# Reordering the start of expert routing in a hybrid attention and PEER kernel: meta gates, two projections, first sorts

## The chip, the cores and the metric

The kernel runs on one core of one Trainium2 chip. The metric is the device time of one execution in microseconds. A profile of one execution goes with it. Engines are named as in the profile: PE (matrix multiplications), DVE (vector), ACT (activations), POOL (which here issues gathers by index and does small arithmetic) and SP (which issues plain DMAs).

## The reference

Two layers over 528 rows (16 meta rows ahead of 512 rows of x), 1024 columns. In each layer a mixer is added to the rows, and then a PEER feed-forward network. The first mixer has stick-breaking attention and a short convolution, the second a windowed mean. What the change touches is the PEER part of the first layer:

```
q = (hb @ w_query).reshape(t, 8, 2, 128)
s = einsum('thpc,phkc->thpk', q, keys)
sv, si = top_k(s, 16)
cand = sv[:, :, 0, :, None] + sv[:, :, 1, None, :]
top_s, top_pos = top_k(cand, 16)
idx, gate = expert numbers of top_pos, softmax(top_s)
act = gelu(einsum('tnd,td->tn', expert_u[idx], hb))
y = einsum('tn,tnd->td', gate * act, expert_v[idx])
```

Each of 528 tokens takes 8 heads times 16 experts, so 128 rows of u and 128 of v, in float32, from tables of 16384 experts in each layer.

## The kernel before, in words

**Tiles and gathers.** There is the meta tile of 16 tokens and four tiles of 128 tokens, in two layers; the meta rows are needed in the first layer only. u and v of an expert lie side by side in memory. One gather (L1736, `gather_pool`, POOL) fetches 128 rows of 8 KB, for a tile u and v of all 128 experts of one token, for the meta rows 8 experts of each of the 16 tokens. There are 16 gathers for the meta rows and 8 times 128 for the tiles, 1040 in all. A chunk is 16 of them (CHUNK, L30). They land in groups of cells, four early ones (`ring_early`) and two late ones (`ring_late`); a group holds 3 x 1024 columns and successive gathers share its middle, so gather n needs the dot of the last user of its group and the sum of the user before that (class Place, L86). While only four groups exist these are gathers n-4 and n-8. The late groups lie in memory that the mixer uses: they may be filled only behind `late_constants` (L599), which waits until all output projections of the mixer are done. It stands behind the 20th gather of tile 0 (EARLY_TILE_ROWS, L80).

**Dots, weights, sums.** For each gather DVE multiplies u with the normed token rows and adds along the row (L2027, `dots_vector`). Four gathers make a batch: gelu of their dots, times the gates, gives weights. For the first nine batches DVE does the arithmetic (L1947 to L1969), with one exponential on ACT (L1917); the weights of a batch come right behind the first dot of the next batch. ACT spreads a weight into columns (L1927, `columns_scalar`), and PE adds v times weight (L1822 for the meta rows, L1861 for tiles; `meta_sums_tensor`, `sums_tensor`).

**The order of the work.** Every engine has one program in order, written by hand; engines wait for each other by semaphores. Work of other kinds is hung into these loops as hooks: a pair (row, step) lets an engine do the step behind its own instruction for that row. Routing one tile takes four pieces of two heads: PE multiplies a query (L1361), ACT copies it (L1368), PE transposes it (L1374), ACT copies (L1379), PE multiplies with the keys (L1452), and DVE sorts in 13 stages (`topk_stages`, L1456 on), the longest being the one-hot comparison (L1534). `piece_indices` (L1567) then writes the expert numbers of the piece, `piece_exponentials` (ACT, L1578) and `piece_gates` (DVE, L1584) make its gates.

**The start, where the change lies.** PE ends the attention and projects the mixer's output in eight half tiles, `project_tensor` 2 to 5 ahead of the meta sums and 6 to 9 step by step as hooks of the meta sums and of tile 0 (`project_step`, L935). DVE adds products 2 and 3 to the rows of tile 0 (L953), ACT takes 4 to 9 (`take_projected`, L957). DVE sorts the meta rows; PE selects by a small multiplication the indices and later the gates of the meta rows into the layout of the gathers (`meta_select_tensor`, L1425); DVE copies them (`meta_indices_vector` L1431, `meta_gates_vector` L1435). The indices go into a corner of one PSUM bank (QUERY_BANK, which query 1 fills later), the gates into another corner of the same bank. Then tile 0 is normed (L1276 to L1298, result hb), transposed (L1354), copied (L1289) and its first two pieces are queried and scored (`first_query`). The first two sorts are hooks of DVE's meta rows and of tile 0, the third and fourth follow as hooks too (META_QUERIED, L2132).

The two programs' lines around the change, PE and DVE before the meta loop:

```
meta_select_tensor(pe, top_i, META_IDX, s_midx)
project_tensor(pe, 3)
project_tensor(pe, 4)
start_tensor(pe, 1, P, 0)
```

```
dots_vector(dve, None, 0, [(0, lambda: meta_gates_vector(dve))] + of_chunk(early, 0) + ...)
```

Of the kernel before, what the change touches and what calls it, by code (L numbers as in the profile page):

```python
# [14 lines left out]
P = 128  # L15
# [102 lines left out]
def program(nc, x, x_T, x_cat, meta_tokens, mixer_small, even_w_in, even_w_out, odd_norm_g, odd_pool_w, odd_pool_scale, ffn_norm_g, peer_w_query,  # L118
# [3 lines left out]
    with ctx:  # L122
# [1300 lines left out]
        META_IDX, META_GATE = QUERY_BANK[:, 0:TOPK], QUERY_BANK[:, TOPK:2 * TOPK]  # L1423
# [615 lines left out]
        def tile_of(slot, n=P):  # L2039
            return hres[0:n, bass.ds(slot, 1), :].rearrange("p a d -> p (a d)")  # L2040
# [92 lines left out]
        SECOND_SORT = 8  # L2133
# [51 lines left out]
        def _(act):  # L2185
# [12 lines left out]
            take_projected(act, 4)  # L2198
            first_query(1)
            take_projected(act, 5)  # L2200
# [24 lines left out]
            def iteration(j, start=()):  # L2225
# [4 lines left out]
            columns_scalar(act, None, 0, [(4, first_indices), (5, lambda: piece_exponentials(act, 0)),   # L2230
                                          (5, lambda: take_projected(act, 6)), (10, lambda: take_projected(act, 7)),
                                          (12, lambda: stage_gates(act, 1, 1))] +
# [3 lines left out]
                  (4, lambda: piece_exponentials(act, 1)), (22, lambda: norm_scalar(act, 2, P, tile_of(1))),  # L2236
# [14 lines left out]
        def _(dve):  # L2251
# [8 lines left out]
            dve.wait_ge(s_meta_rows, 1)  # L2260
            logits_vector(dve, 0, P, 2)
            dve.wait_ge(s_v_in, HEAD_PAIRS)
            meta_indices_vector(dve)
            gates_vector(dve, 0, P, 2)
# [8 lines left out]
            def iteration(j, layer, start=()):  # L2273
# [5 lines left out]
            early = ([(i // 2, first[i]) for i in range(TOPK_STAGES)] + [(7, lambda: piece_indices(dve, 0))] +  # L2279
# [3 lines left out]
            dots_vector(dve, None, 0, [(0, lambda: meta_gates_vector(dve))] + of_chunk(early, 0) + [(11, lambda: piece_gates(dve, 0))])  # L2283
            tile(0, [(at - CHUNK, f) for at, f in early if at >= CHUNK] +
                 [(9, lambda: piece_gates(dve, 1)), (28, lambda: norm_vector(dve, 2, P, tile_of(1), 0)),
# [13 lines left out]
        def _(pe):  # L2299
# [5 lines left out]
            meta_select_tensor(pe, top_i, META_IDX, s_midx)  # L2305
            project_tensor(pe, 3)
            project_tensor(pe, 4)
# [3 lines left out]
            def first_query(s):  # L2311
                query_tensor(pe, first_piece(1) + s, s, P, 0, KD, (LATE_BANK, QUERY_BANK)[s])
                if s == 0:
                    pe.wait_ge(s_gate, 1)
                    meta_select_tensor(pe, soft, META_GATE, s_gateT)
                queryT_tensor(pe, first_piece(1) + s, P)
                pe.wait_ge(s_read, first_piece(1) + s)
                scores_tensor(pe, first_piece(1) + s, s, P)
            first_query(0)
            pe.wait_ge(s_idx, 1)  # L2320
            pe.wait_ge(s_mgate, 1)
            first_query(1)
            project_tensor(pe, 5)
# [59 lines left out]
```

## Time and profile before

| | |
|---|---|
| median of 3 runs | 3003.5 us (3002.41 to 3005.78) |
| the profiled execution | 3006.1 us, of which the span shown is 3004.3 us |
| PE, DVE, POOL, ACT busy | 63%, 62%, 46%, 27% of the span |
| moved by DMA | 1140 MB, of which 1091 MB by the gathers |
| mean granted clock of PE | 0.775 of full speed |

The time of an execution is a little more than the span between its first and last instruction on the engines. The profile counts us from the start of the span. A share of busy time is a mean over stages of different kinds: a table by stretches, and timelines of single engines, tell where something waits. In a timeline the last bracket of a line is how long the engine sat idle ahead of it and who released it. Merged lines give the number of instructions (x). Numbers of the weight loads of PE (PEld) lie beside its multiplications.

### The profile page before, as it was taken

How to read it: one execution, taken by the hardware profiler on the slowest of the kernel's cores; microseconds unless marked ns; L12 is line 12 of the kernel's file. 1: busy time of each engine (PE TensorE's matmuls, PEld its weight loads, DVE VectorE, ACT ScalarE, POOL GpSimd, SP SyncE). 2: the span in 40 equal slices, each digit the busy share in tenths (PEclk: the TensorE clock that was granted, in tenths of full speed). 3: DMA queues.
4: the chain of work that ended last, by engine and by line, in shares of the span. 5: the costliest groups of instructions: out<-in, count | busy, mean ns of one | idle time of the engine just before them, and what ended most of it. 6: DMA issues, size and time to landing. Idle time of an engine off the chain costs nothing. (4 is left out here: it accounts for less than half of the span.)

```text
span 3004.3 us, 41799 instructions
## 1 busy us (share of the span) xinstructions
PE 1888.3 (63%) x13330; PEld 765.0 (25%) x13330; DVE 1858.6 (62%) x4622; ACT 810.2 (27%) x3258; POOL 1369.0 (46%) x2651
## 2 busy tenths in 40 slices
PE   9999866746664566455665566566655666444444
PEld 4774322212221222122222222222222222111111
DVE  2155667885776567565776567755776477644444
ACT  2033122223222222123222332232223322232223
POOL 0100235555555555345555554555555555545554
PEclk9999988877876687777786777777777777666665
DMA  5132689999999999999999999999999999999998
GB/s 193 62 133 112 219 344 418 420 420 421 417 410 421 419 419 420 416 403 421 420 419 414 414 421 419 417 407 421 420 419 405 421 420 416 420 421 420 421 419 336
DMA packets 165496, 1140.19 MB, mean 380 GB/s; under 512 B 18672, under 2 KB 19696, under 8 KB 29856
## 3 DMA queue, kind: packets, MB, share of 16 engines
q0 software_dynamic: 149760, 1090.59, 88.1%
q1 hardware_dynamic: 15520, 46.94, 4.1%
q8 instruction: 109, 1.79, 0.2%
q14 instruction: 107, 0.88, 0.1%
HBM read 1135.30 MB, written 2.10 MB: 379 GB/s over the span
## 5 line engine op out<-in xcount | busy, mean ns | idle before, releaser
L2027 DVE SCALAR_TENSOR_TENSOR ring_early<-ring_early,psum 128x1024 f32<-128x1024 f32 x704 | 857.9, 1219 | 611.8 <-DMA ring_early<-in_peer_uv,idx_u 299.2
L1861 PE MATMUL psum<-ring_early,w_col 128*32 128x256 f32 x5504 | 541.2, 499 | 717.0 <-ACT w_col L1927 636.1
L2027 DVE SCALAR_TENSOR_TENSOR ring_late<-ring_late,psum 128x1024 f32<-128x1024 f32 x336 | 409.4, 1218 | 304.9 <-DMA ring_late<-in_peer_uv,idx_u 157.3
L1736 POOL DMA_INDIRECT ring_early<-in_peer_vu,idx_u x352 | 343.9, 977 | 468.3 <-DVE ring_early L2027 150.0
L1736 POOL DMA_INDIRECT ring_early<-in_peer_uv,idx_u x352 | 344.1, 978 | 427.9 <-DVE ring_early L2027 155.4
L1861 PE MATMUL psum<-ring_late,w_col 128*32 128x256 f32 x2688 | 271.3, 499 | 365.0 <-ACT w_col L1927 329.6
L1861 PEld LDWEIGHTS psum<-ring_early,w_col 128*32 128x32 f32 x5504 | 191.4, 133 | 1104.1 <-issue 737.8
L1919 ACT ACTIVATE ge<-ga 128x4 f32<-128x4 f32 (+2 forms) x256 | 52.5, 205 | 1403.9 <-POOL ga L1985 1403.9
L1927 ACT ACTIVATE w_col<-block_fold,weight 128x32 f32<-128x32 f32 x1024 | 268.9, 313 | 421.3 <-POOL weight L2001 395.4
L1361 PE MATMUL psum<-wq,hbT 128*128 128x512 f32 x512 | 314.7, 704 | 1.2 <-ACT hbT L1289 1.2
L1736 POOL DMA_INDIRECT ring_late<-in_peer_vu,idx_u x168 | 160.3, 954 | 267.7 <-PE psum L1861 152.2
L1861 PEld LDWEIGHTS psum<-ring_late,w_col 128*32 128x32 f32 x2688 | 93.4, 133 | 551.9 <-issue 343.7
L1736 POOL DMA_INDIRECT ring_late<-in_peer_uv,idx_u x168 | 168.3, 1002 | 113.6 <-issue 73.8
L1334 PE MATMUL psum<-hb_b,ident 128*32 128x512 f32 x768 | 152.5, 931 | 0.0
L1334 PE MATMUL psum<-hb,ident 128*32 128x512 f32 x768 | 138.4, 853 | 0.0
L1361 PEld LDWEIGHTS psum<-wq,hbT 128*128 128x128 f32 x512 | 84.9, 205 | 121.0 <-issue 119.6
L1902 ACT COPY gate_u<-gateT 32x8 f32<-32x8 f32 x512 | 99.1, 194 | 11.7
L1890 ACT COPY idx_u<-idxT 32x8 uint32<-32x8 uint32 x512 | 99.1, 194 | 11.6
L1083 POOL COPY vs<-qkv 128x640 f32<-128x640 f32 x4 | 2.9, 730 | 216.5 <-PE psum L760 122.6
L1334 PE MATMUL psum<-hres,ident 128*32 128x512 f32 x512 | 93.2, 861 | 0.0
L890 PE MATMUL psum<-hT,w_ring 128*128 128x264 f32 x384 | 87.0, 388 | 1.7 <-ACT qkv L989 1.7
L890 PEld LDWEIGHTS psum<-hT,w_ring 128*128 128x128 f32 x384 | 72.5, 190 | 15.0 <-ACT qkv L989 2.0
(294 smaller groups left out, 2221.4 us busy)
## 6 DMA issues: line engine op xcount, KB each, us to landing
wq<-in_peer_w_query SPq DMA_DIRECT2D x16, 1024.0 KB, 17.8
w_ring<-in_even_w_in SPq DMA_DIRECT2D x5, 2048.0 KB, 8.0
ring_early<-in_peer_vu,idx_u POOLq DMA_INDIRECT x352
ring_early<-in_peer_uv,idx_u POOLq DMA_INDIRECT x352
w_ring<-in_even_w_out SPq DMA_DIRECT2D x1, 4096.0 KB, 13.0
ring_late<-in_peer_vu,idx_u POOLq DMA_INDIRECT x168
ring_late<-in_peer_uv,idx_u POOLq DMA_INDIRECT x168
hT<-in_x_T SPq DMA_DIRECT2D x4, 528.0 KB, 6.7
```

The source lines that it names most:

```text
L890: last = nc.tensor.matmul(psum[:, 4 + 2 * (i % 2) + half, 0:HALF], w, hT[:, k, HALF * half:HALF * half + HALF], start=(k == 0), stop=(k == ...
L1083: nc.gpsimd.tensor_copy(vs[pair % 2][:, :, :], qkv[:, :, 2, 2 * DH * pair:2 * DH * pair + 2 * DH]).then_inc(s_v_in, 1)
L1334: nc.tensor.matmul(rows_for((f + 1) % 2)[BLOCK * g:BLOCK * g + BLOCK, c], ident[:, BLOCK * b:BLOCK * b + BLOCK], hb_of(job)[:, c], start=T ...
L1361: ins = nc.tensor.matmul(dst[0:n, :], hbT[:, k, 0:n], wq[:, k, bass.ts(s, 512)], start=(k == 0), stop=(k == KD - 1))
L1736: nc.gpsimd.indirect_dma_start(pair_cells(at), None, uv_rows if at.side else vu_rows, bass.IndirectOffsetOnAxis(idx_u[par][:, i:i + 1], 0) ...
L1861: nc.tensor.matmul(block_part(b, n), w_col[:, i % W_SLOTS, :], v_cell(at)[:, part_cols(n)], start=False, stop=last, skip_group_check=True) ...
L1890: nc.scalar.copy(cell, entry).then_inc(s_idx_u, 1)
L1902: nc.scalar.copy(cell, entry).then_inc(s_gate_u, 1)
L1919: nc.scalar.activation(ge[:, 0:n], ga[:, 0:n], ACT.Exp, scale=-GELU_B).then_inc(s_gact, 1)
L1927: nc.scalar.activation(w_col[:, i % W_SLOTS, 0:base.shape[-1]], base[:, :], ACT.Copy, scale=weight[par][:, i:i + 1]).then_inc(s_wcol, 1)
L2027: nc.vector.scalar_tensor_tensor(out=cell, in0=cell, scalar=1.0, in1=rows, op0=ALU.mult, op1=ALU.mult, accum_out=dot[par][:, i:i + 1]).the ...
```

## The change

It does six things. The gates of the meta rows go into the corner of the bank LATE_BANK. PE selects them right behind the indices, ahead of project 3, instead of in query 0 of tile 0, and waits for their copy ahead of query 0 instead of ahead of query 1. DVE makes the meta gates ahead of the copy of the indices and copies them right behind it, ahead of its additions, instead of as a hook of meta row 0; a wait for the repeated meta rows is dropped ahead of the logits (it stands again ahead of the dots). Project 4, which stood ahead of the transposes of tile 0, goes behind query 1, ahead of project 5; on ACT the two takings go from among the queries into the hooks of meta rows 0 and 1. DVE's first sort begins at row 3 instead of 0, and the second at 11 instead of 8. The hooks that hang on these sorts (the indices of tile 0's first chunk on ACT, exponentials and gates of pieces 0 and 1, staging of the gates) go some rows later.

```diff
--- before.py
+++ after.py
@@ -1420,7 +1420,7 @@
             act.wait_ge(s_q_ps, 1)
             nc.scalar.copy(q_T[:, :, :], FB.rearrange("p (a n) -> p a n", a=LISTS)).then_inc(s_qT, 1)
 
-        META_IDX, META_GATE = QUERY_BANK[:, 0:TOPK], QUERY_BANK[:, TOPK:2 * TOPK]
+        META_IDX, META_GATE = QUERY_BANK[:, 0:TOPK], LATE_BANK[:, 0:TOPK]
 
         def meta_select_tensor(pe, table, dst, done):
 
@@ -2130,7 +2130,8 @@
                     (at + 30, lambda: norm_vector(dve, job, P, src, 1))]
 
         META_QUERIED = (13, 29)
-        SECOND_SORT = 8
+        FIRST_SORT = 3
+        SECOND_SORT = FIRST_SORT + 8
         FIRST_QUERIED = (36, 50, 64, 78)
         FIRST_START = 92
 
@@ -2195,9 +2196,7 @@
             norm_scalar(act, 1, P, tile_of(0))
             transposed_scalar(act, 1, P)
             first_query(0)
-            take_projected(act, 4)
             first_query(1)
-            take_projected(act, 5)
 
             def first_indices():
                 act.wait_ge(s_piece, 1)
@@ -2227,13 +2226,14 @@
 
             act.wait_ge(s_setup, SETUP_STEPS)
             early = routing_scalar(act, 1, META_QUERIED, 2)
-            columns_scalar(act, None, 0, [(4, first_indices), (5, lambda: piece_exponentials(act, 0)), 
+            columns_scalar(act, None, 0, [(0, lambda: take_projected(act, 4)), (1, lambda: take_projected(act, 5)),
+                                          (7, first_indices), (9, lambda: piece_exponentials(act, 0)),
                                           (5, lambda: take_projected(act, 6)), (10, lambda: take_projected(act, 7)),
-                                          (12, lambda: stage_gates(act, 1, 1))] +
+                                          (15, lambda: stage_gates(act, 1, 1))] +
                            of_chunk(early, 0))
             tile(0, [(at - CHUNK, f) for at, f in early if at >= CHUNK] +
                  [(4, lambda: take_projected(act, 8)), (14, lambda: take_projected(act, 9)),
-                  (4, lambda: piece_exponentials(act, 1)), (22, lambda: norm_scalar(act, 2, P, tile_of(1))),
+                  (8, lambda: piece_exponentials(act, 1)), (22, lambda: norm_scalar(act, 2, P, tile_of(1))),
                   (24, lambda: piece_exponentials(act, 2)), (28, lambda: transposed_scalar(act, 2, P)),
                   (30, lambda: pool_norm_scalar(act, 0, 3, META, META_ROWS)),
                   (40, lambda: piece_exponentials(act, 3))] +
@@ -2257,11 +2257,11 @@
 
             for stage in topk_stages(dve, 0, 0, P, meta=True):
                 stage()
-            dve.wait_ge(s_meta_rows, 1)
             logits_vector(dve, 0, P, 2)
+            gates_vector(dve, 0, P, 2)
             dve.wait_ge(s_v_in, HEAD_PAIRS)
             meta_indices_vector(dve)
-            gates_vector(dve, 0, P, 2)
+            meta_gates_vector(dve)
             add_projected(dve, 2)
             add_projected(dve, 3)
             norm_vector(dve, 1, P, tile_of(0), 0)
@@ -2276,13 +2276,13 @@
             dve.wait_ge(s_meta_rows, 1)
             first = topk_stages(dve, first_piece(1), 0, P)
             second = topk_stages(dve, first_piece(1) + 1, 1, P)
-            early = ([(i // 2, first[i]) for i in range(TOPK_STAGES)] + [(7, lambda: piece_indices(dve, 0))] +
+            early = ([(FIRST_SORT + i // 2, first[i]) for i in range(TOPK_STAGES)] + [(FIRST_SORT + 7, lambda: piece_indices(dve, 0))] +
                      [(SECOND_SORT + i, second[i]) for i in range(TOPK_STAGES)] +
                      [(SECOND_SORT + TOPK_STAGES, lambda: piece_indices(dve, 1))] +
                      routing_vector(dve, 1, META_QUERIED, 2, piece_indices))
-            dots_vector(dve, None, 0, [(0, lambda: meta_gates_vector(dve))] + of_chunk(early, 0) + [(11, lambda: piece_gates(dve, 0))])
+            dots_vector(dve, None, 0, of_chunk(early, 0) + [(15, lambda: piece_gates(dve, 0))])
             tile(0, [(at - CHUNK, f) for at, f in early if at >= CHUNK] +
-                 [(9, lambda: piece_gates(dve, 1)), (28, lambda: norm_vector(dve, 2, P, tile_of(1), 0)),
+                 [(13, lambda: piece_gates(dve, 1)), (28, lambda: norm_vector(dve, 2, P, tile_of(1), 0)),
                   (32, lambda: piece_gates(dve, 2)), (37, lambda: pool_norm_vector(dve, 0, META, META_ROWS)),
                   (47, lambda: piece_gates(dve, 3))] +
                  routing_vector(dve, 2, FIRST_QUERIED) + tables_hooks(dve, 2, 0, 107) +
@@ -2303,23 +2303,22 @@
             meta_rows_tensor(pe)
             pe.wait_ge(s_routed, 2)
             meta_select_tensor(pe, top_i, META_IDX, s_midx)
+            pe.wait_ge(s_gate, 1)
+            meta_select_tensor(pe, soft, META_GATE, s_gateT)
             project_tensor(pe, 3)
-            project_tensor(pe, 4)
             start_tensor(pe, 1, P, 0)
             pe.wait_ge(s_hbT, 4)
 
             def first_query(s):
                 query_tensor(pe, first_piece(1) + s, s, P, 0, KD, (LATE_BANK, QUERY_BANK)[s])
-                if s == 0:
-                    pe.wait_ge(s_gate, 1)
-                    meta_select_tensor(pe, soft, META_GATE, s_gateT)
                 queryT_tensor(pe, first_piece(1) + s, P)
                 pe.wait_ge(s_read, first_piece(1) + s)
                 scores_tensor(pe, first_piece(1) + s, s, P)
+            pe.wait_ge(s_mgate, 1)
             first_query(0)
             pe.wait_ge(s_idx, 1)
-            pe.wait_ge(s_mgate, 1)
             first_query(1)
+            project_tensor(pe, 4)
             project_tensor(pe, 5)
 
             def tile(j, hooks):
```

## Rows read from the trace of the kernel before

**Rows 1.** The page's slices of the span, DMA's share in tenths.
```profile
DMA  5132689999999999999999999999999999999998
```

**Rows 2.** Stretches: busy us (count) of PE, PEld, DVE, ACT, POOL; clock, DMA, GB/s.
```profile
287.00:290.40 3.40, 3.40 (x6) 1.38 (x5) 0.46 (x1) 0.00 (x0) 2.23 (x3) 0.51 0.26 55
372.86:374.60 1.74, 1.74 (x17) 0.42 (x16) 1.71 (x9) 0.00 (x0) 0.86 (x1) 1.00 0.97 344
396.30:399.60 3.30, 3.30 (x24) 0.99 (x17) 2.43 (x6) 0.99 (x5) 0.95 (x1) 0.50 0.79 320
422.00:429.00 7.00, 6.54 (x54) 2.01 (x52) 5.37 (x18) 1.01 (x3) 1.89 (x2) 1.00 0.16 32
500.00:2990.00 2490.00, 1444.56 (x11024) 534.31 (x11012) 1606.27 (x3893) 685.15 (x2939) 1279.60 (x2487) 0.74 1.01 417
```

**Rows 3.** Timeline of POOL, 287 to 427: start, us, instruction, idle before and releaser.
```profile
287.56 1.20 POOL L1736 DMA_INDIRECT ring_early<-in_peer_vu,idx_u  x1 [53.64 <-ACT idx_u L1887]
...
301.57 0.94 POOL L1736 DMA_INDIRECT ring_early<-in_peer_uv,idx_u  x1 [9.08 <-DVE ring_early L2027]
...
321.30 0.94 POOL L1736 DMA_INDIRECT ring_early<-in_peer_uv,idx_u  x1 [18.80 <-DVE ring_early L2027]
...
337.15 1.17 POOL L1736 DMA_INDIRECT ring_early<-in_peer_vu,idx_u  x1 [9.10 <-PE psum L1822]
...
348.58 0.94 POOL L1736 DMA_INDIRECT ring_early<-in_peer_uv,idx_u  x1 [2.71 <-DVE ring_early L2027]
...
361.79 0.94 POOL L1736 DMA_INDIRECT ring_early<-in_peer_vu,idx_u  x1 [3.99 <-DVE ring_early L2027]
...
426.96 0.95 POOL L603 MEMSET prev<- 128x1024 f32 x1 [8.73 <-PE psum L944]
```

**Rows 4.** Timeline of PE, 285 to 426: merged runs of instructions.
```profile
285.44 0.62 PE L1428 MATMUL psum<-top_i,sel 128*128 128x16 f32 x4
285.91 8.81 PE L930 MATMUL psum<-w_ring,catT 128*128 128x512 f32 x16
...
303.33 1.04 PE L1354 MATMUL psum<-ident,hb 128*128 128x128 f32 x8
...
325.95 1.02 PE L928 MATMUL psum<-hres,ident 128*128 128x512 f32 x2
...
333.77 0.62 PE L1830 MATMUL psum<-hres,ident 16*16 16x256 f32 x8
...
335.67 0.62 PE L1822 MATMUL psum<-ring_early,w_col 128*16 128x256 f32 x8 [1.28 <-ACT w_col L1927]
...
347.10 0.63 PE L1822 MATMUL psum<-ring_early,w_col 128*16 128x256 f32 x8 [1.48 <-ACT w_col L1927]
...
360.21 0.63 PE L1822 MATMUL psum<-ring_early,w_col 128*16 128x256 f32 x8 [1.45 <-ACT w_col L1927]
...
395.71 0.64 PE L1861 MATMUL psum<-ring_early,w_col 128*32 128x256 f32 x8 [4.27 <-ACT w_col L1927]
396.14 3.58 PE L1334 MATMUL psum<-hb,ident 128*32 128x512 f32 x16
...
422.63 1.92 PE L1334 MATMUL psum<-hb,ident 128*32 128x512 f32 x16
...
425.88 1.02 PE L944 MATMUL psum<-w_ring,catT 128*128 128x512 f32 x2
```

**Rows 5.** Timeline of DVE, 286 to 358.
```profile
286.67 0.19 DVE L1613 TENSOR_TENSOR soft<-soft,soft_r 128x32 f32<-128x32 f32 x1
...
298.25 1.28 DVE L1298 SCALAR_TENSOR_TENSOR hb<-hres,rstd,ffn_g 128x1024 f32<-128x1024 f32 x1
...
313.05 0.17 DVE L1437 COPY gateT<-psum 128x16 f32<-128x16 f32 x1 [12.26 <-PE psum L1428]
...
319.30 1.22 DVE L2027 SCALAR_TENSOR_TENSOR ring_early<-ring_early,psum 128x1024 f32<-128x1024 f32 x1
...
357.93 1.22 DVE L2027 SCALAR_TENSOR_TENSOR ring_early<-ring_early,psum 128x1024 f32<-128x1024 f32 x1 [1.78 <-DMA ring_early<-in_peer_uv,idx_u]
```

## The prediction

> **What bounds the kernel now.** I read the slices of the page first. DMA is busy at 9 tenths from slice 7 to the end and nothing else is, so the expert rows that are fetched set the time there [rows 1]. A table of busy time by stretch says the same: from 500 to 2990 us the DMA engines move 417 GB/s at a share of 1.01 [rows 2]. Each gather brings 128 rows of 8 KB, 1.049 MB, so one takes 1.049 / 417 = 2.51 us there, and whatever happens to DVE, PE or POOL in that stretch costs nothing as long as the queue stays full. A change before it can only move the moment from which the queue is full. That moment is visible: from 422 to 429 DMA works at a share of 0.16, and in the timeline of POOL the last thing before the full stretch is the MEMSET of L603 at 426.96, which waited 8.73 us for PE L944, the last output projection [rows 2, 3]. Behind it 1004 of the 1040 gathers follow at the DMA's own pace (36 are issued before it). So the question is one number: how much earlier or later does PE finish that last product (425.88 + 1.02 = 426.9 [rows 4])? A shift there goes 1:1 into the time.
>
> I number gathers, dots and sums 0 to 15 for the meta rows and 16 on for tile 0. Gather n needs dot n-4 and sum n-8 (four cell groups). In POOL's timeline gather 4 is issued at 301.57, gather 5 waits 18.80 us for dot 1, gather 8 waits 9.10 us for PE's sum 0, and from there the gathers keep going [rows 3]. Dot 1 is late because DVE, right after dot 0, sits 12.26 us for the meta gates of PE and then does two stages of the first sort, until 319.30 [rows 5].
>
> **The change, part by part.**
> *Meta gates earlier.* PE does the second selection right behind the first. It now waits for the gates: their last DVE operation ended at 286.67 + 0.19 = 286.86, with the index copy ahead of it, and without that copy some 0.3 us sooner (two DVE operations of this size, 0.19 each), so 286.5 to 286.6 [rows 5]. Queued behind that wait on PE is project 3, which began at 285.91 [rows 4]. Selecting four matmuls costs 0.62 [rows 4], so project 3 begins at about 287.15, **+1.24**. The index copy itself goes behind the gates, at most 0.7 later, and with it gathers 0 to 3; dot 0 comes at about 300.8, some 13 us behind the first issue, so this is covered. Were it not, it would cost those 0.7.
>
> *DVE's wait goes.* Meta gates are copied near 287.3, so the 12.26 us are gone, and with the first sort moved to row 3, dots 1 to 3 follow dot 0 at 1.22 each. Gathers 5 to 7 are issued before 308 instead of at 321.30 and after. What is late next: gather 8, for sum 0. So these 18.80 us are worth nothing by themselves; their gain is only what they save behind gather 8.
>
> *The projections.* Before, project 4 ran while DVE and ACT made the normed rows of tile 0 (hb, ready at 298.25 + 1.28 = 299.53), and PE came to the transposes at 303.33 [rows 4, 5]. Now PE comes to them when hb is ready: 299.53 + 1.24 + 0.1 = 300.85. From the transposes to the start of project 5 the rows have 325.95 - 303.33 = 22.62 us; the selection inside it lay beside ACT's copy and its removal gives nothing. So the two queries end at 323.47, and now *two* projections follow, each as long as project 5 was, 333.77 - 325.95 = 7.82. The meta sum is opened (0.62, its last 0.06 under the next) at 339.1 and **sum 0 comes at 339.7 instead of 335.67: +4.0** [rows 4]. ACT's weights column 0 is ready long before, since it no longer stands behind project 5.
>
> *What of it is made up.* Between sum 0 and sum 8 PE waited 1.48 us at 347.10 and 1.45 at 360.21 for weights that needed dots 8 and 12 [rows 4]. PE without these waits needs 24.54 - 2.93 = 21.6, so sum 8 comes no sooner than 361.3, **+1.1**: the lower end. Upper end, if the row that dot 12 needs lands as slowly as before: sum 4 at 339.7 + 11.43 - 1.48 = 349.65, gather 12 behind it by 1.48 at 351.13, landing 357.93 - 348.58 = 9.35, and from dot 12 to sum 8 2.28: 362.8, +2.55 [rows 3 to 5]. I take +1.1, because the gathers before it now come at PE's even pace, 9.95 / 4 = 2.49 us a row, close to the DMA's own 2.51. From sum 8 on PE runs without a wait over its products and fills to the end of the meta rows; the next batches hang on landings of rows that hang on these sums. I take their spacing as before, so the shift stays.
>
> *The sorts.* First sort: its stages run while PE projects, when DVE has nothing else before row 8 lands. Second sort, three rows later: three stages fall into rows 20 to 22, where no sort stood. The longest stage takes 1.74 us [rows 2]. I cost it at nothing: dots there wait for landings. If that cover is gone, 3 x 1.74 = 5.2 at most. The moved exponentials and staged gates of tile 0 wait for nothing later than their new rows, and the ACT work of 1.7 us now behind row 15 lies beside PE's sum 15.
>
> *TensorE's clock.* The change makes PE idle: project 3 ends near 296.0, hb comes at 300.85, 4.9 us. The rows show such a case: after an idle of 4.27 us before 395.71 the granted clock was 0.50 from 396.30 to 399.60, which is the 1.2 GHz level, and the fill took 3.58 us where the one at 422.63 took 1.92 [rows 2, 4]. That is **+1.66** on the path, since transposes and query 0 follow directly. The bounds are 0 and that. I take it, 4.9 being longer than 4.27. The same table has a second fall: 0.51 from 287.00 to 290.40, inside project 3 (8.81 us), though PE had begun it at 285.91 and was busy in all of that stretch [rows 2, 4]. I leave 8.81 as it stands.
> The Trainium skill, in "TensorE: Matmul & The Clock Gate", section "Part 1: The HAM clock gate", gives the slow level to an idle engine and the full one to a busy one, and says that the point of change varies from run to run. Where the engine falls behind an idle stretch the trace agrees (0.50 after 4.27 us); the fall at 287.00 behind issued work it does not explain. By the page alone project 3 would run at full clock, 7.1 instead of 8.81, and the sum would be 1.7 lower.
>
> **Sum:** +1.1 + 1.66 = +2.8 us. The profiled execution has a span of 3004.3 and a time of 3006.1, 2.6 above the median of 3003.5; the shift is put on the median: **3006.3**.
>
> **Rivals.**
> - *The clock does not cost it* (no fall in the gap, or full clock in project 3 because PE's pattern differs): 1.7 less, 3004.6. For it: the fall at 287.00 came without an idle stretch, so the place of falls is not fixed. The page's rule above would give this time through project 3.
> - *Hidden anyway:* later batches have slack of 3 us and the gate stays at 426.9. For it: PE waits 4.27 at 395.71. Against it: that wait is for a landing of a row issued behind these sums. 3003.5.
> - *Faster batches:* from gather 8 at 337.15 to the MEMSET at 426.96, 28 gathers take 89.8 us, 3.2 each against 2.51, so a batch of four at full DMA pace saves 2.8 [rows 3]. If the freed DVE lets two batches do so: 4.0 - 5.6 = -1.6, 3001.9. With four: -7.2, 2996.3. Against it: the waits there are round trips (9.35 for a landing), not DVE work.
> - *Slower, by the second sort on DVE in rows 20 to 22:* +2.8 + 5.2 = +8.0, 3011.5. It decides as soon as dots 21 to 23 start behind a stage and not behind DMA. Before, dots of this stretch came behind DMA.
>
> **How the numbers follow.** A measurement of this kernel can tell about 0.2%, 6.0 us, from no change; that is 2997.5 to 3009.5. Forecast 0.45, clock 0.20, hidden 0.16, faster batches 0.09 (a third of it past 0.2%), slower 0.10. Of the forecast's cases with the upper landing bound (3007.8) a little also passes 3009.5 by scatter of the runs (3002.41 to 3005.78). So faster 0.04, same 0.86, slower 0.10. The range holds forecast with both bounds, clock, hidden and the two-batch case with the scatter: 3000.5 to 3010.0.
>
> **What would show it.** Right: gathers 5 to 7 issued before 310; PE idle some 5 us before the transposes of tile 0, and a half clock behind it; project 4 and 5 back to back and sum 0 near 339.7 to 341.4; the MEMSET of L603 near 429.7; 417 GB/s behind it. Wrong: a MEMSET before 426 (batches faster), or past 432 with dots 21 to 23 released by DVE itself; or a DMA that is not full behind the MEMSET, since then the end does not follow that point at all.

## The result and the profile after

| | before | after |
|---|---|---|
| median of 20 runs each | 3003.9 us (3000.16 to 3006.35) | 3008.68 us (3006.80 to 3011.34) |
| ratio, 95% interval | | 1.0018 (1.0012 to 1.0024) |
| profiled execution, its span | 3006.1, 3004.3 | 3007.9, 3006.1 |

The change costs 4.8 us, 0.18%; the interval reaches from 3.6 to 7.2 us. That lies within the 0.2% that the prediction called no change, at its edge, and inside its range; by the interval it is a loss and not a gain.

The timeline of POOL in the changed kernel, which answers to [rows 3]:

```profile
303.46 0.94 POOL L1736 DMA_INDIRECT ring_early<-in_peer_uv,idx_u  x1 [9.96 <-DVE ring_early L2027]
304.70 0.94 POOL L1736 DMA_INDIRECT ring_early<-in_peer_uv,idx_u  x1 [0.30 <-issue]
...
307.18 0.94 POOL L1736 DMA_INDIRECT ring_early<-in_peer_uv,idx_u  x1 [0.30 <-issue]
344.48 0.93 POOL L1736 DMA_INDIRECT ring_early<-in_peer_vu,idx_u  x1 [36.36 <-PE psum L1822]
...
366.05 0.93 POOL L1736 DMA_INDIRECT ring_early<-in_peer_vu,idx_u  x1 [2.49 <-PE psum L1822]
...
429.07 0.95 POOL L603 MEMSET prev<- 128x1024 f32 x1 [9.14 <-PE psum L944]
```

Gathers 4 to 7 now follow each other at 1.24 us, with no wait for another engine; the 18.80 us are gone. In their place gather 8 waits 36.36 us for PE, and it is issued at 344.48 instead of 337.15. Gather 16 is late by 4.3, the MEMSET by 2.1. All times of this run lie some 0.7 later from the start: the repetition of the meta rows on PE (L1444), ahead of everything that was changed, begins at 284.17 here and at 283.49 before. Below, times of different runs are compared from that instruction. In the kernel before it stands here, with query 0 of tile 0:

```profile
283.49 1.98 PE L1444 MATMUL psum<-ring_early,spread 16*128 16x512 f32 x4
...
305.53 7.13 PE L1361 MATMUL psum<-wq,hbT 128*128 128x512 f32 x16 [1.16 <-ACT hbT L1289]
```

The timeline of PE in the changed kernel, against [rows 4]:

```profile
284.17 1.98 PE L1444 MATMUL psum<-ring_early,spread 16*128 16x512 f32 x4
...
287.33 0.62 PE L1428 MATMUL psum<-soft,sel 128*128 128x16 f32 x4 [0.58 <-DVE soft L1613]
287.80 8.81 PE L930 MATMUL psum<-w_ring,catT 128*128 128x512 f32 x16
301.48 1.67 PE L1354 MATMUL psum<-ident,hb 128*128 128x128 f32 x8 [4.87 <-DVE hb L1298]
304.31 9.28 PE L1361 MATMUL psum<-wq,hbT 128*128 128x512 f32 x16 [1.16 <-ACT hbT L1289]
...
334.61 1.02 PE L928 MATMUL psum<-hres,ident 128*128 128x512 f32 x2
...
342.43 0.62 PE L1830 MATMUL psum<-hres,ident 16*16 16x256 f32 x8
342.98 0.62 PE L1822 MATMUL psum<-ring_early,w_col 128*16 128x256 f32 x8
...
352.86 0.62 PE L1822 MATMUL psum<-ring_early,w_col 128*16 128x256 f32 x8
...
364.45 0.62 PE L1822 MATMUL psum<-ring_early,w_col 128*16 128x256 f32 x8
...
398.50 0.64 PE L1861 MATMUL psum<-ring_early,w_col 128*32 128x256 f32 x8 [2.17 <-ACT w_col L1927]
```

The second selection waits 0.58 and project 3 begins 3.63 us behind L1444 instead of 2.42. Then the idle stretch, 4.87 us ahead of the transposes, and behind it transposes of 1.67 us (1.04 before) and a query 0 of 9.28 (7.13). Two projections stand ahead of the meta sums. Sum 0 begins 58.81 us behind L1444 instead of 52.18, **6.6 later**. The waits ahead of sums 4 and 8 (1.48 and 1.45 before) are gone.

The timeline of DVE in the changed kernel, against [rows 5]:

```profile
287.99 0.17 DVE L1437 COPY gateT<-psum 128x16 f32<-128x16 f32 x1 [0.62 <-PE psum L1428]
...
302.60 1.22 DVE L2027 SCALAR_TENSOR_TENSOR ring_early<-ring_early,psum 128x1024 f32<-128x1024 f32 x1
...
316.99 0.89 DVE L1511 MAX8 sv<-psum 128x8 f32<-128x128 f32 x4 [10.12 <-PE psum L1452]
...
325.90 0.17 DVE L1963 TENSOR_SCALAR ge<-ge 128x4 f32<-128x4 f32 x1 [4.37 <-ACT ge L1917]
...
349.93 1.22 DVE L2027 SCALAR_TENSOR_TENSOR ring_early<-ring_early,psum 128x1024 f32<-128x1024 f32 x1 [10.81 <-DMA ring_early<-in_peer_vu,idx_u]
...
389.44 1.21 DVE L2027 SCALAR_TENSOR_TENSOR ring_early<-ring_early,psum 128x1024 f32<-128x1024 f32 x1
...
394.25 1.21 DVE L2027 SCALAR_TENSOR_TENSOR ring_early<-ring_early,psum 128x1024 f32<-128x1024 f32 x1
```

Meta gates are copied at 287.99 instead of 313.05, and dot 1 comes at 302.60 instead of 319.30. DVE then waits where it did not wait before: 10.12 us for the scores of the first piece, 4.37 for ACT's first exponential, and 10.81 for the row of gather 8, which hangs on PE. The time that the dots won is spent waiting. The two last lines are dots 21 and 23: DVE had no idle time ahead of them, nor ahead of dot 22 between them, for they start behind stages of the second sort. In the kernel before dot 21 waited for its row:

```profile
384.85 1.22 DVE L2027 SCALAR_TENSOR_TENSOR ring_early<-ring_early,psum 128x1024 f32<-128x1024 f32 x1 [1.84 <-DMA ring_early<-in_peer_uv,idx_u]
```

The busy time by stretch of the changed kernel, columns as in [rows 2]:

```profile
296.70:301.40 4.70, 0.00 (x0) 0.00 (x0) 2.59 (x7) 1.65 (x4) 0.00 (x0) 1.00 0.98 404
301.90:308.60 6.70, 5.54 (x12) 2.68 (x10) 4.87 (x11) 1.07 (x2) 3.74 (x4) 0.50 0.54 171
...
500.00:2990.00 2490.00, 1446.86 (x11025) 536.88 (x11020) 1606.10 (x3892) 685.37 (x2939) 1277.51 (x2487) 0.74 1.01 418
```

PE does nothing from 296.7 to 301.4, and its granted clock is 0.50 from 301.9 to 308.6, the 1.2 GHz level. From 500 us on DMA moves 418 GB/s at a share of 1.01, where it was 417 and 1.01 before.

### The profile page after: what moved, and what is told of

It is laid out like the page before. It is cut to its first block and busy times, and to the rows that moved or that the text cites. A ratio compares the mean times of both kernels' runs of the same rounds, so it can differ in the third digit from the quotient of the medians.

```text
span 3006.1 us, 41797 instructions
## 1 busy us (share of the span) xinstructions
PE 1892.0 (63%) x13330; PEld 768.6 (26%) x13330; DVE 1858.8 (62%) x4622; ACT 810.5 (27%) x3258; POOL 1366.2 (45%) x2651
## 5 line engine op out<-in xcount | busy, mean ns | idle before, releaser
L1736 POOL DMA_INDIRECT ring_early<-in_peer_vu,idx_u x352 | 342.3, 973 | 492.8 <-PE psum L1861 156.2
L890 PE MATMUL psum<-hT,w_ring 128*128 128x264 f32 x384 | 87.0, 388 | 1.7 <-ACT qkv L989 1.7
L890 PEld LDWEIGHTS psum<-hT,w_ring 128*128 128x128 f32 x384 | 72.5, 190 | 15.0 <-ACT qkv L989 2.0
## 6 DMA issues: line engine op xcount, KB each, us to landing
w_ring<-in_even_w_out SPq DMA_DIRECT2D x1, 4096.0 KB, 12.9
```

The costliest lines, as they stand in the source:

```text
L890: last = nc.tensor.matmul(psum[:, 4 + 2 * (i % 2) + half, 0:HALF], w, hT[:, k, HALF * half:HALF * half + HALF], start=(k == 0), stop=(k == ...
L1736: nc.gpsimd.indirect_dma_start(pair_cells(at), None, uv_rows if at.side else vu_rows, bass.IndirectOffsetOnAxis(idx_u[par][:, i:i + 1], 0) ...
```

## The experiments

The theory going in: only the moment at which PE ends the last projection counts; the change makes it later by moving project 4 behind the queries, through the longer way to sum 0 and through the slow clock behind the idle stretch. Rivals: the later sorts slow DVE's batches; PE's wait for the gates ahead of project 3 is the loss.

**Project 4 ahead of the transposes again.** The changed kernel, on PE:

```diff
             project_tensor(pe, 3)
+            project_tensor(pe, 4)
             start_tensor(pe, 1, P, 0)
...
             first_query(1)
-            project_tensor(pe, 4)
             project_tensor(pe, 5)
```

> The changed kernel with project 4 alone put back ahead of the transposes of tile 0; the early gates and the late sorts stay. Theory (PE's order): the 4.87 us of idle PE and the slow clock behind it are gone, sum 0 comes near 336 to 337 instead of 343, the dots no longer hold anything up, so the MEMSET of L603 comes at 424 to 427.5 and the time is 3000 to 3004, that is 4.5 to 8.5 us under the changed kernel. Rival 1 (the late second sort slows the batches on DVE): the time stays within 1.5 us of 3008.7. Rival 2 (PE's wait for the gates ahead of project 3, +1.2): it stays 1 to 2 above before, 3005 to 3006.

Measured: 3001.6 us, ratio to before 0.9996 (0.9987 to 1.0005), so 7.1 under the changed kernel's 3008.7. The timelines of PE and of POOL:

```profile
305.18 1.04 PE L1354 MATMUL psum<-ident,hb 128*128 128x128 f32 x8
307.38 7.13 PE L1361 MATMUL psum<-wq,hbT 128*128 128x512 f32 x16 [1.16 <-ACT hbT L1289]
...
336.18 0.63 PE L1822 MATMUL psum<-ring_early,w_col 128*16 128x256 f32 x8
```

```profile
422.49 0.95 POOL L603 MEMSET prev<- 128x1024 f32 x1 [8.17 <-PE psum L944]
```

Transposes and query have their old durations, sum 0 comes 52.06 us behind L1444, and the MEMSET comes at 422.49. Early gates and late sorts are in this kernel, and the takings on ACT; together they do not make it slower than before. So neither rival is the cause of the loss. What the gates cost by themselves, which the takings hide here, is told below.

**Only project 4 moved.** The kernel before with this (ACT's two takings go with it, since query 1 and project 4 would else wait for each other):

```diff
-            take_projected(act, 4)
...
-            take_projected(act, 5)
...
-            columns_scalar(act, None, 0, [(4, first_indices), (5, lambda: piece_exponentials(act, 0)), 
+            columns_scalar(act, None, 0, [(0, lambda: take_projected(act, 4)), (1, lambda: take_projected(act, 5)),
+                                          (4, first_indices), (5, lambda: piece_exponentials(act, 0)),
...
-            project_tensor(pe, 4)
             start_tensor(pe, 1, P, 0)
...
             first_query(1)
+            project_tensor(pe, 4)
             project_tensor(pe, 5)
```

> The kernel before with project 4 alone moved behind query 1 (and its taking and that of project 5 moved on ACT); gates and sorts as before. Theory (PE's order): PE idles near 4.9 us behind project 3, the clock falls behind it, sum 0 comes at 339 to 342 and the time is 3006 to 3009. Rival 1 (sorts) and rival 2 (gates): neither is in this kernel, so 3003 to 3004.5.

Measured: 3006.5 us, 1.0012 (1.0003 to 1.0021). On PE:

```profile
300.20 1.97 PE L1354 MATMUL psum<-ident,hb 128*128 128x128 f32 x8 [4.87 <-DVE hb L1298]
303.33 9.45 PE L1361 MATMUL psum<-wq,hbT 128*128 128x512 f32 x16 [1.16 <-ACT hbT L1289]
```

PE idles 4.87 us, transposes and query take 1.97 and 9.45, sum 0 comes 58.07 behind L1444. That is 3.3 above before in the same comparison, without early gates and late sorts; the share of ACT's takings in it is seen below.

**The idle stretch filled.** The changed kernel with multiplications whose result nobody reads:

```diff
             project_tensor(pe, 3)
+            for k in range(5):
+                nc.tensor.matmul(FA, catT[:, k, META:META + P], w_out_sb[:, k, 0:512], start=True, stop=True)
             start_tensor(pe, 1, P, 0)
```

> The changed kernel with five multiplications of 128x512, whose result nobody reads, put into PE's idle stretch ahead of the transposes (some 4.4 us of work in 4.9 of idle). Only the clock behind the gap can change. Theory: the clock stays full, transposes and query 0 take 1.04 and 7.1 us instead of 1.67 and 9.28, sum 0 comes 2 to 2.8 us sooner and the time is 3006 to 3007. Rival (the clock costs nothing on the path): 3008 to 3009.5, as the changed kernel.

Measured: 3006.5 us, 1.0013 (1.0004 to 1.0022), 2.2 under the changed kernel and 2.3 under the next version, which has the changed kernel's time and ran in the same comparison. The same stretches and the way to sum 0:

```profile
296.70:301.40 4.70, 4.18 (x10) 1.52 (x8) 2.59 (x7) 1.65 (x4) 0.00 (x0) 1.00 1.01 415
301.90:308.60 6.70, 5.54 (x18) 2.67 (x17) 4.84 (x11) 1.07 (x2) 3.75 (x4) 1.00 0.54 177
```

```profile
301.45 1.09 PE L1354 MATMUL psum<-ident,hb 128*128 128x128 f32 x8 [0.57 <-DVE hb L1298]
303.71 7.13 PE L1361 MATMUL psum<-wq,hbT 128*128 128x512 f32 x16 [1.16 <-ACT hbT L1289]
...
340.23 0.62 PE L1822 MATMUL psum<-ring_early,w_col 128*16 128x256 f32 x8
```

With 4.18 us of work in the gap the clock is 1.00 behind it, the transposes take 1.09 and the query 7.13, and sum 0 comes 56.09 us behind L1444 instead of 58.81: the slow clock is 2.7 of the 6.6. The intervals of the two ratios overlap, so the time alone would not show it; the trace does. The rest of the 6.6 is project 4's place.

**Sorts and their hooks back.** The changed kernel with `FIRST_SORT = 0`, and the hooks that hang on it at their rows of before (4, 5 and 12 of the meta rows and 4 of tile 0 on ACT, 11 and 9 on DVE).

```diff
-        FIRST_SORT = 3
+        FIRST_SORT = 0
```

> The changed kernel with the first sort back at row 0, the second at row 8 and their hooks back where they were; gates and projections as changed. Theory (PE's order): dots 1 to 3 wait for the scores again, some 18 us, gathers 5 to 7 come near 320 and later, but gather 8 still waits for sum 0 near 343: the time stays within 1.5 us of the changed kernel, 3007 to 3010. Rival 1 (the late second sort): 3 us or more sooner, 3003 to 3005.5.

Measured: 3008.8 us, 1.0020 (1.0011 to 1.0029): the changed kernel's time. The timeline of POOL:

```profile
304.40 0.94 POOL L1736 DMA_INDIRECT ring_early<-in_peer_uv,idx_u  x1 [9.96 <-DVE ring_early L2027]
323.47 0.94 POOL L1736 DMA_INDIRECT ring_early<-in_peer_uv,idx_u  x1 [18.14 <-DVE ring_early L2027]
...
345.70 0.94 POOL L1736 DMA_INDIRECT ring_early<-in_peer_vu,idx_u  x1 [15.48 <-PE psum L1822]
```

Gather 5 waits 18.14 us again, and it costs nothing, since gather 8 still waits 15.48 for PE. The 18.80 us that the change removed were worth nothing, as the prediction had it.

**Project 4 cut into steps.** The changed kernel, with project 4's nine steps in PE's idle places. By its edit this version, and the version with gates in the idle stretch, multiplies tile 0's columns and rows there in place of tile 1's, in the same shapes; so it does not compute the kernel's result, and its time is that of the order alone.

`fourth(n)` issues one of them: the identity on the rows for n = 0, then one of the eight products.

```diff
             project_tensor(pe, 3)
+            for n in range(4):
+                fourth(n)
             start_tensor(pe, 1, P, 0)
+            fourth(4)
             pe.wait_ge(s_hbT, 4)
...
                 query_tensor(pe, first_piece(1) + s, s, P, 0, KD, (LATE_BANK, QUERY_BANK)[s])
+                fourth(5 + 2 * s)
                 queryT_tensor(pe, first_piece(1) + s, P)
+                fourth(6 + 2 * s)
...
-            project_tensor(pe, 4)
             project_tensor(pe, 5)
```

> The changed kernel with project 4 cut into its nine steps and put into PE's idle places: four steps while tile 0 is normed, one while ACT copies the transposes, one in each of the four waits of the two queries. Theory (only the start of the meta sums, and with it the MEMSET, sets the time): PE idles nowhere over 1 us, the clock stays full, sum 0 comes near 332.5 to 333.5 where project 4 ahead of the transposes gave 336.2, and the time is 2997 to 2999.5, the lowest so far. Rival (from there on DVE's sorts or the landings limit the batches, so an earlier sum 0 is worth nothing): 3001 to 3002, as with project 4 ahead of the transposes.

Measured: 2998.5 us, 0.9987 (0.9978 to 0.9996), with sum 0 48.37 us behind L1444, 3.7 sooner than with project 4 ahead of the transposes. The median is 2.7 to 3.1 under the two versions with project 4 ahead (3001.2 further down, 3001.6): an earlier sum 0 is worth most of its time, and nothing on DVE or in the landings takes its place yet.

**Project 4 ahead, sorts back.** The first experiment and the fourth together, so that of the change the early gates and ACT's takings are left.

```diff
             project_tensor(pe, 3)
+            project_tensor(pe, 4)
             start_tensor(pe, 1, P, 0)
...
-        FIRST_SORT = 3
+        FIRST_SORT = 0
```

> The changed kernel with project 4 ahead of the transposes and both sorts back at rows 0 and 8, so that the gates' early selection is what is left of the change (and the takings on ACT). Theory: dots 1 to 3 wait for the scores again, gathers 5 to 7 come after 320, and with sum 0 near 336 DVE's sort stages and dots of rows 5 to 8 now stand behind the weights: gathers 9 to 12 come later than with late sorts, 3003 to 3005. Rival (the sorts' place is worth nothing, whatever sum 0 does): 3001 to 3002.5, as with project 4 ahead and late sorts.

Measured: 3001.2 us, 0.9996 (0.9987 to 1.0005). The theory missed and the rival held: with sum 0 at its old place too, the place of the sorts is worth nothing that can be told (0.4 us apart). Gathers 5 to 7 come at 322.94 to 328.76, and gather 8 still waits 7.76 us for PE.

**Gates in the idle stretch.** As the version in steps, with the second selection behind project 3 and DVE's copy of the gates behind its second addition.

```diff
-            pe.wait_ge(s_gate, 1)
-            meta_select_tensor(pe, soft, META_GATE, s_gateT)
             project_tensor(pe, 3)
+            pe.wait_ge(s_gate, 1)
+            meta_select_tensor(pe, soft, META_GATE, s_gateT)
...
-            meta_gates_vector(dve)
             add_projected(dve, 2)
             add_projected(dve, 3)
+            meta_gates_vector(dve)
```

> As the version with project 4 in steps, but PE selects the meta gates behind project 3, in the idle stretch, and DVE copies them behind its second addition. Theory: PE's wait for the gates no longer stands ahead of project 3, which begins 1.2 us sooner, and the rest follows: 1.0 to 1.5 us under the version with project 4 in steps, 2996 to 2998.5. Rival (the 1.2 us are given back to the DMA or to ACT's norm): no difference, within 0.5.

Measured: 2995.9 us, 0.9977 (0.9968 to 0.9986), 2.6 under the version in steps where 1.0 to 1.5 was expected. Sum 0 comes 2.9 us sooner (45.48 behind L1444). 1.2 of it is the wait; the other 1.7 is a project 3 of 7.11 us instead of 8.81, as in the next.

**The same with tile 1's columns.** The wait for the rows of x goes to tile 1's with them.

```diff
-                    nc.tensor.matmul(late_bank(4), ident[:, :], hres[:, 0, 0:512], start=True, stop=False)
+                    nc.tensor.matmul(late_bank(4), ident[:, :], hres[:, 1, 0:512], start=True, stop=False)
...
-                ins = nc.tensor.matmul(late_bank(4), catT[:, n - 1, cols_of(0)], ...
+                ins = nc.tensor.matmul(late_bank(4), catT[:, n - 1, cols_of(1)], ...
```

> The version with the meta gates selected behind project 3 and project 4 in steps, now with tile 1's columns in project 4's steps (the two versions in steps above multiplied tile 0's there, in the same shapes). Theory: as measured with tile 0's columns, 2994 to 2998, the fastest kernel here, since only the start of the meta sums counts. Rival (the values matter for the time, by other expert numbers fetched): 3 us or more away from 2995.9.

Measured: 2996.4 us, 0.9977 (0.9968 to 0.9986): faster than both kernels, 12.3 under the changed one. The columns make no difference that can be told (2995.9 with tile 0's). The version in steps was not run again with tile 1's. The timelines of PE and of POOL:

```profile
284.29 1.98 PE L1444 MATMUL psum<-ring_early,spread 16*128 16x512 f32 x4
...
286.74 7.11 PE L930 MATMUL psum<-w_ring,catT 128*128 128x512 f32 x16
...
298.71 1.09 PE L1354 MATMUL psum<-ident,hb 128*128 128x128 f32 x8 [0.38 <-DVE hb L1298]
```

```profile
418.00 0.95 POOL L603 MEMSET prev<- 128x1024 f32 x1 [8.74 <-PE psum L944]
```

PE waits 0.38 us for the normed rows, project 3 runs 7.11 us, and the MEMSET comes at 418.00, 11 us ahead of the changed kernel's.

**Only ACT's takings moved.** The kernel before with the ACT part of the second experiment's diff, and nothing else.

```diff
-            take_projected(act, 4)
...
-            take_projected(act, 5)
...
-            columns_scalar(act, None, 0, [(4, first_indices), (5, lambda: piece_exponentials(act, 0)), 
+            columns_scalar(act, None, 0, [(0, lambda: take_projected(act, 4)), (1, lambda: take_projected(act, 5)),
+                                          (4, first_indices), (5, lambda: piece_exponentials(act, 0)),
```

> The kernel before with one thing changed: ACT takes projects 4 and 5 behind the weight columns of rows 0 and 1 instead of among the queries; gates, projections and sorts as before. Theory (what the changed kernel makes up behind sum 0 comes from ACT's first exponential, which stood behind project 5): sum 0 follows the opening at 334.4 instead of 335.67, PE no longer waits at sums 4 and 8, the MEMSET comes 87 to 88 us behind sum 0 instead of 91.3, and the time is 2999 to 3001.5. Rival (it comes from the early gates): 3002.5 to 3004, as before.

Measured: 2999.5 us, 0.9983 (0.9974 to 0.9992). In the kernel before, ACT stood here:

```profile
333.88 0.59 ACT L959 COPY hres<-psum 128x512 f32<-128x512 f32 x1 [9.04 <-PE psum L930]
334.36 0.21 ACT L1917 ACTIVATE ge<-ga 128x4 f32<-128x4 f32 x1
```

It waited 9.04 us for project 5, took it, and only then came to the exponential. Now the timelines of ACT and of PE:

```profile
326.63 0.21 ACT L1917 ACTIVATE ge<-ga 128x4 f32<-128x4 f32 x1 [2.21 <-DVE ga L1953]
330.70 0.31 ACT L1927 ACTIVATE w_col<-fold,weight 128x16 f32<-128x16 f32 x1 [3.86 <-DVE weight L1969]
330.91 0.56 ACT L959 COPY hres<-psum 128x512 f32<-128x512 f32 x1
```

```profile
333.35 0.62 PE L1830 MATMUL psum<-hres,ident 16*16 16x256 f32 x8
333.90 0.63 PE L1822 MATMUL psum<-ring_early,w_col 128*16 128x256 f32 x8
```

ACT's first exponential comes at 326.63 instead of 334.36, the first weight column is ready at 331.0, and sum 0 follows the opening of the meta sum without the 1.28 us of before: 50.85 us behind L1444 instead of 52.18. From sum 0 to sum 8 it takes 21.8 us where the two profiles of the kernel before took 24.5 and 23.7. This small part of the change, which the prediction named in half a sentence, is the only part of it tried here that gains, 3.7 us of the medians.

**Both kernels once more,** for a second profile of each.

> The kernel before once more, for a second profile. Theory: 2577 us from the MEMSET of L603 to the end of the span, 90 to 92 us from sum 0 to the MEMSET, with waits of PE ahead of sums 4 and 8. Rival (the 91.3 of the first profile was a slow clock behind an idle stretch): 87 to 89.

> The changed kernel once more, for a second profile. Theory: the time follows the MEMSET of L603 by a fixed distance, 2577 us to the end of the span; with the common start of the run taken off, PE idles 4.9 us, the clock is half for 6 to 7 us behind it, sum 0 comes near 342 to 343.

Measured, one time each: 3002.1 us for the kernel before and 3011.3 for the changed one. From the second profile of the kernel before, PE and POOL:

```profile
335.57 0.62 PE L1822 MATMUL psum<-ring_early,w_col 128*16 128x256 f32 x8 [1.28 <-ACT w_col L1927]
```

```profile
423.28 0.95 POOL L603 MEMSET prev<- 128x1024 f32 x1 [6.85 <-PE psum L944]
```

And from the second profile of the changed kernel:

```profile
400.55 1.08 PE L1861 MATMUL psum<-ring_early,w_col 128*32 128x256 f32 x8 [5.03 <-ACT w_col L1927]
```

```profile
431.19 0.95 POOL L603 MEMSET prev<- 128x1024 f32 x1 [8.16 <-PE psum L944]
```

From the MEMSET to the end of the span it is 2577.0 and 2578.3 us. In the kernel before it took 91.3 us from sum 0 to the MEMSET in the first profile and 87.7 in the second, so the rival's number held: the first profile was a long one. Its cause did not: the fill behind the idle stretch was slow in both (3.58 and 3.32 us against 1.92), and most of the 3.6 us lies behind it. In the changed kernel it took 86.1 and 88.5. There the difference lies behind the meta rows: PE waited 2.17 us for the first batch of tile 0 in the one (398.50 in its timeline above) and ran its next fill in 1.93; in the other it waited 5.03, and the fill took 3.00.

All profiles together, in us (sum 0 is counted from the start of L1444; the last column is the median of the runs):

| kernel | sum 0 | sum 0 to MEMSET | MEMSET to end of span | median |
|---|---|---|---|---|
| before, two profiles | 52.18, 52.20 | 91.3, 87.7 | 2577.3, 2577.0 | 3003.9 |
| only takings moved | 50.85 | 86.8 | 2577.7 | 2999.5 |
| project 4 ahead, sorts back | 52.05 | 87.6 | 2576.5 | 3001.2 |
| project 4 ahead | 52.06 | 86.3 | 2577.9 | 3001.6 |
| only project 4 moved (with takings) | 58.07 | 86.2 | 2577.1 | 3006.5 |
| changed, gap filled | 56.09 | 88.0 | 2576.7 | 3006.5 |
| changed, sorts back | 59.10 | 89.1 | 2577.1 | 3008.8 |
| changed, two profiles | 58.81, 58.74 | 86.1, 88.5 | 2577.0, 2578.3 | 3008.7 |
| project 4 in steps | 48.37 | 88.3 | 2577.0 | 2998.5 |
| and gates in the gap, tile 0's columns | 45.48 | 86.8 | 2576.4 | 2995.9 |
| and gates in the gap, tile 1's columns | 45.47 | 88.2 | 2577.2 | 2996.4 |

The medians come from four comparisons, in which the kernel before had 3002.8 to 3003.9; a difference under 1 us between rows says little.

Behind the MEMSET every kernel takes 2577 us within 1.3. Ahead of it, the ten kernels with the takings moved go with sum 0, over a width of 13.6 us against 12.9 of the medians: the median less sum 0 is 2948.4 to 2951.0. The kernel before lies above them at 2951.7; it waits 2.9 and 2.1 us ahead of sums 4 and 8 in its two profiles, the ten others 0.2 at most.

One thing ahead of L1444 is not explained. It begins at 283.9 to 285.1 in the nine profiles of kernels with the gates moved and at 283.0 to 284.1 in the other four. The difference is there at 100 us, long before any of the changed work (PE's L890 begins at 100.13 before and at 100.81 changed). Whether it is chance stays open; it is in the times and not in the column of sum 0.

Taken one after the other, by the medians of 11 to 20 runs, the parts of the change are: takings on ACT 3003.9 to 2999.5 (-4.4 against the 20 runs, -3.7 in its own comparison), early gates +1.7 (2999.5 to 3001.2), late sorts +0.4, which is nothing that can be told, and project 4 behind the queries +7.1, of which the slow clock is 2.2. In one order such parts add up of themselves. Another order checks them: project 4 costs 7.1 without gates and sorts too (2999.5 to 3006.5), the gates 2.3 with project 4 behind the queries (3006.5 to 3008.8), the sorts nothing there either (3008.8 and 3008.7). For the gates the intervals of the ratios overlap; what speaks for them is sum 0, 1.2 and 1.0 us later in the two pairs.

## Why the prediction was right or wrong

It was right in direction and in its range; the likeliest value, +2.8 us, was low against +4.8 (3.6 to 7.2). The mechanism was right: PE's order on the way to sum 0, and a MEMSET that follows it. One term was too small, and what the change gains came from a part that the sum did not price by itself.

- *The end follows the MEMSET of L603 1:1.* Right: 2577 us in thirteen profiles.
- *Meta gates earlier, +1.24 on project 3.* Right: 3.63 - 2.42 = 1.21. The experiment with project 4 ahead and sorts back against the one with takings alone gives 1.7 us of time for it, with sum 0 later by 1.2.
- *DVE's wait of 12.26 us goes and is worth nothing.* Right, shown by the sorts put back: 3008.8 with an 18.14 us wait of gather 5, 3008.7 without.
- *Two projections ahead of the meta sum, sum 0 +4.0.* Right: without the slow clock, with the gap filled, sum 0 is 56.09 - 52.18 = 3.9 later.
- *An idle stretch of 4.9 us, +1.66 for the clock.* The stretch was right (4.87). **This is the term that was mis-sized:** the slow clock cost 0.63 on the transposes and 2.15 on the query, 2.8 us, and filling the gap gave 2.7 of sum 0 and 2.2 of the time back. In the three other profiles with this gap the two cost 2.7 to 3.3. The price was taken from a row where the clock was half for 3.3 us behind the gap; here it was half from 301.9 to 308.6. Behind the gap PE does the short transposes and then idles another 1.16 us for ACT's copy; the clock returned only under query 0. In the row that gave the price a long fill had followed at once. That this second wait kept the clock low was not tried. The row itself was one of several outcomes: in the thirteen profiles this fill took 2.81 to 3.58 us behind waits of 2.91 to 5.03 us in ten, and 1.93 behind waits of 1.66, 2.17 and 3.21 us in three. So the price of 1.66 was the highest that the fill shows, and still too low for the other place.
- *Made up between sum 0 and sum 8, 2.9.* Right: 21.5 us against 24.5 (23.7 in the second profile of the kernel before), predicted 21.6. The prediction gave it to PE's back-to-back rows. The version with only the takings moved, 21.8, shows where it comes from: ACT's first exponential no longer stands behind project 5.
- *The rest of the way stays as before.* On average right, but the profile of before was a long one just there (91.3 us from sum 0 to the MEMSET, 87.7 in the second). The comparison of single profiles, +2.1 at the MEMSET, is therefore smaller than that of the medians. With 6.6 at sum 0, and 23.7 and 24.5 us from there to sum 8 before against 21.5 after, the profiles give 3.6 to 4.4; with the clock at its measured 2.8 the prediction's own sum is 1.1 + 2.8 = 3.9. From L1444 to the MEMSET the two profiles of each kernel have 141.7 before and 146.1 changed in the mean, +4.4.
- *Rivals.* The clock costing nothing (3004.6), hidden (3003.5) and faster batches (3001.9) did not come. From sum 0 to the MEMSET it took 86 to 89 us in all profiles but the first, the second of the kernel before among them, so the batches went no faster for the freed DVE. The slower rival's sign did come: dots 21 to 23 start behind sort stages (389.44 to 394.25 above), where the kernel before waited 1.3 to 1.8 us for DMA ahead of each. Its cost did not: dot 24 begins 53.2 us behind sum 0, and 53.6 with the sorts back; the times are 3008.7 against 3008.8, and 3001.6 against 3001.2 with project 4 ahead. The stages took the place of waits, as the prediction had assumed; the sign was badly chosen. (The rows that gained a stage are 21 to 23 by the diff, not 20 to 22.)
- *Its other signs.* Gathers 5 to 7 before 310, the idle stretch with a half clock behind it, projects 4 and 5 back to back and 418 GB/s at the end: all came. Sum 0 did not come at 339.7 to 341.4 but at 342.98, 342.3 with the later start taken off: that is the clock term. The MEMSET at 429.07, near the 429.7 that was named, is luck: a later start and a dearer clock stand against a profile of before that was long behind sum 0. The second profile has it at 431.19.
- *The page's rule on the clock.* The Trainium skill, in "TensorE: Matmul & The Clock Gate", section "Part 1: The HAM clock gate", gives the slow level to an idle engine. The trace agrees for the gap: with it filled, the clock stayed at 1.00. For project 3 the measurement stays at odds with it as the prediction said: about 8.8 us in all profiles but two, with and without a short wait ahead of it. In the two versions with gates in the gap it took 7.11, at a granted clock of 1.00 where the kernel before had 0.51, though what PE does ahead of it is there what the kernel before does. That the point of change varies from run to run, as the section says, would allow for this; what sets it here stays open.

## What to carry to other kernels

Before taking a wait away, ask what the waiting engine's next customer is waiting for: the largest wait between the gathers, 18.80 us, was worth nothing, because gather 8 hung on another engine, and a part of the change that the prediction did not price by itself, two copies moved on ACT, was worth 3.7 us. Work that stands ahead of a wait may be filling that wait: project 4 looked like an obstacle ahead of the transposes, and it was the filling of PE's idle stretch; here, cutting it into steps that fit the gaps beat both orders. And the clock behind a gap on TensorE is priced from a gap with the like work behind it: two gaps of nearly the same length, 4.27 and 4.87 us, cost 1.7 and 2.8 us here. A sum against a single profile inherits what that profile has of its own: here 3.6 us between sum 0 and the MEMSET.

## What was not expected of the hardware

- The clock stayed at half for 6.7 us behind one idle stretch of 4.87 us (0.50 from 301.9 to 308.6), where 3.3 us stood behind one of 4.27 in the kernel before.
- The scatter of the runs, 6.2 us from lowest to highest before and 4.5 changed, has a part of its own between the meta rows and the MEMSET: waits of 2.17 to 5.03 us of PE at the first batch of tile 0, with fills of 1.93 or 3.00 us behind them, in two profiles of the same kernel.
- Project 3 took 8.73 to 8.81 us in eleven profiles and 7.11 in two; in those two the instructions on PE ahead of it are the same as in the kernel before.
